# A constant's root ahead of the last boundary's first square, and a last tile stored in two halves

## The chip, the cores and the metric

The program runs on one core of a Trainium2 chip. The core has five engines that the text names: TensorE (PE in the profile, its weight loads PEld), VectorE (DVE), ScalarE (ACT), GpSimd (POOL) and SyncE (SP), which here only issues transfers. Each engine works through its own list of instructions in order; engines wait for one another by semaphores. The metric is the device time of one execution in microseconds; the time of a kernel is the median of several runs.

## The reference

Three transformer layers for one sequence of 512 tokens of width 1024 in float32: two layers with attention, a dense part and a gated embedding, then a third one whose dense part and closing normalisation are what the change lies in.

```python
def rmsnorm(x, g):
    xf = x.astype(jnp.float32)
    y = xf * lax.rsqrt(jnp.mean(xf * xf, axis=-1, keepdims=True) + NORM_EPS_2)
    return (y * g.astype(jnp.float32)).astype(x.dtype)
...
        x = x + mixed
        h2 = rmsnorm(x, norm2_g[l])
        ffn = (jax.nn.silu(h2 @ w_ffn_gate[l]) * (h2 @ w_ffn_up[l])) @ w_ffn_down[l]
        x = x + ffn
    return rmsnorm(x, norm_f_g)
```

## The kernel before

The tokens lie in four tiles of 128 (`t` = 0 to 3); `X[:, t, :]` holds the residual of tile t, one token in each partition and 1024 features in a row. All weights come in one stream of 302 chunks of 512 KB. SP loads a chunk into `RW` (L490), POOL cuts it into a high part `WH` (L529) and a low part `WL` (L532), and TensorE multiplies in three passes for each product (`mm3`, L652: high by high, high by low, low by high). Every product of the program runs through line L643.

The last stage is the downward projection of the third layer (`down`, L921): 22 chunks, one for each 128 hidden features. Its weights operand is the hidden tile (`HSH`, `HSL`, two slots each, cut by VectorE at L1688 and L1689), its moving operand the chunk. Each chunk adds to all eight banks of `PS`, two banks for each token tile. The last two chunks are treated apart (`wide_end`, L727): TensorE ends the sums of tile 0, then those of tile 1, then tile 2 with both chunks, then tile 3 with both chunks. It raises `tile_done` after each of tiles 0 to 2 and `chunk_used` after tile 3.

Then follows boundary 7, the closing normalisation, on ACT and VectorE at once. For each tile:

- VectorE adds the banks to the residual (`residual`, L1590) and raises `var_ready`;
- ACT squares the tile and sums the squares into `MV` (L2107), then takes the root of the mean square plus a small constant into `STD` (L2108), and raises `std_ready`. ACT computes functions from tables; the built program puts an instruction ACT_TABLE_LOAD where a function needs another table than the one in place. The function in use ahead of boundary 7 is Silu (L2267, in `gate`);
- VectorE takes the reciprocal of the root (`scale`, L1596), multiplies the tile by it and by the gain row `G` in place in `X` (`normed_tile`, L1610), and raises `y_ready`;
- SP waits for `y_ready` and stores the tile of 512 KB to `out` (L516); at the end it waits until all stores have landed.

VectorE's list is: residual 0, residual 1, scale 0, residual 2, scale 1, residual 3, scale 2, scale 3. ACT's is: square and root of tile 0, of tile 1, of tile 2, of tile 3.

Tiles in on-chip memory are laid out in the order in which they are declared. `X`, `XTH`, `XTL` (the operands of most other products), `RW`, `WH`, `WL` and the constants up to `IDLE` come first. `EPS`, `GAINS` and all tiles of the stages (`G`, `HT`, `HSH`, `HSL`, `OH`, `SWH`, `TWH` and others) come after `IDLE`. The built program of before puts `XTH` at byte 32,896 of each partition, `WH` at 82,048, `EPS` at 103,552, `SWH` at 108,416, `HSH` at 182,144, `HSL` at 186,240, `OH` at 209,120 and `TWH` at 217,312.

Of the kernel before, what the change touches and what calls it, by code (L numbers as in the profile page):

```python
# [26 lines left out]
P = 128  # L27
S = 512
T = S // P
D = 1024  # L30
KD = D // P
UNIT = 512
# [142 lines left out]
def program(nc, d, out):  # L175
    ctx = ExitStack()
    with ctx:
        def sb(name, shape, dt=F32, at=ctx):
            return at.enter_context(nc.sbuf_tensor(name, shape, dt))
# [5 lines left out]
        X = sb("X", [P, T, D])  # L185
# [9 lines left out]
        TRI_R = sb("TRI_R", [P, P], F32R)  # L195
        CHUNKTRI_R = sb("CHUNKTRI_R", [P, P], F32R)
        IDLE = sb("IDLE", [P, P], F32R)
        EPS = sb("EPS", [P, 2])
        GAINS = sb("GAINS", [P, 7, KD])
        BIASES = sb("BIASES", [P, 4, KD])  # L200
# [76 lines left out]
        G = sb("G", [P, 2, D], at=dense)  # L277
# [82 lines left out]
        def probs(h):  # L360
# [74 lines left out]
        y_ready = sem("y_ready")  # L435
# [36 lines left out]
        out_stored = sem("out_stored")  # L472
# [7 lines left out]

        BOUND = [(True, "layer", 0), (True, "layer", 1), (False, None, None), (True, "layer", 2),
                 (True, "layer", 3), (False, "rms", 4), (True, "rms", 5), (True, "rms", 6)]
        Y_BASE = [0, 4, 8, 12, 16, 20, 20, 20]

        @block.sync
        def _(sp):
            def load(i, j):
                if j >= RAW:
                    sp.wait_ge(lo_split, j - RAW + 1 + RAW * i)
                sp.dma_start(RW[:, j % RAW, :], d["stream"][RAW * i + j]).then_inc(landed[j % RAW], 16)  # L490


            sp.dma_start(RW[:, 0, 0:UNIT], d["stream"][0][:, 0:UNIT]).then_inc(half_landed, 16)
            sp.dma_start(RW[:, 0, UNIT:], d["stream"][0][:, UNIT:]).then_inc(landed[0], 16)
            for j in range(1, RAW):
                if j >= 2:
                    sp.wait_ge(xs_landed[j - 2], 16)
                load(0, j)
            def load_row(h):
                if h == FOX0:  # L500
                    sp.wait_ge(rows_stored, 16)
                if h >= FOX0 + 2:
                    sp.wait_ge(masked, 4 * (h - 1))
                src = d["gate_rows"][h - FOX0:h - FOX0 + 1, :].to_broadcast([P, S])
                sp.dma_start(BC[:, h % 2, :], src).then_inc(bc_landed[h % 2], 16)

            over_chunks(sp, RAW, FIRST["fox"] + 19, load)
            load_row(FOX0)
            load_row(FOX0 + 1)
            over_chunks(sp, FIRST["fox"] + 19, FIRST["out1"] + RAW, load)  # L510
            for h in range(FOX0 + 2, FOX0 + FOX_H):
                load_row(h)
            over_chunks(sp, FIRST["out1"] + RAW, CHUNKS, load)
            for t in range(T):
                sp.wait_ge(y_ready, Y_BASE[7] + t + 1)
                sp.dma_start(out[:, t, :], X[:, t, :]).then_inc(out_stored, 16)  # L516
            sp.wait_ge(out_stored, 16 * T)


        @block.gpsimd  # L520
# [832 lines left out]
        def _(ve):  # L1353
            own = Order(ve, ve_own)
            M, A, SUB, MAX, MIN = ALU.mult, ALU.add, ALU.subtract, ALU.max, ALU.min
# [13 lines left out]
            for j in range(1, 4):  # L1369
                w = slice(2 * j, 2 * j + 2)  # L1370
# [31 lines left out]
            for t in range(T):  # L1402
                x = ve.bn_stats(CBN[:, T + t, :], CQ[:, t, Q_LORA:])
            own(x)
            for j in range(8):
                x = ve.bn_aggr(CMV[:, j, :], CBN[:, j, :])
# [5 lines left out]
            for j in range(8):  # L1412
                w = slice(0, Q_LORA) if j < T else slice(Q_LORA, Q_LORA + KV_LORA)
                x = ve.tensor_scalar(CQ[:, j % T, w], CQ[:, j % T, w], CRS[:, j:j + 1], None, M)
# [157 lines left out]
            def boundary(b, end, embedding_layer=None):  # L1572
                add, kind, n = BOUND[b]
                layer = kind == "layer"

                def residual(t):
                    if add:
                        if t < T - 1:
                            ve.wait_ge(tile_done, 3 * added[0] + t + 1)
                        else:  # L1580
                            ve.wait_ge(chunk_used, end)
                        a = ALPHA if layer else 1.0
                        if layer:
                            sums = PSF[:, D * t:D * (t + 1)]
                            own(ve.scalar_tensor_tensor(sums, X[:, t, :], a, sums, M, A,  # L1585
                                                        accum_out=MV[:, t, 0:1]))
                            ve.tensor_scalar(MV[:, t, 0:1], MV[:, t, 0:1], -1.0 / D, None,
                                             M).then_inc(var_ready, 1)
                        else:
                            ve.scalar_tensor_tensor(X[:, t, :], X[:, t, :], a, PSF[:, D * t:D * (t + 1)],  # L1590
                                                    M, A).then_inc(var_ready, 1)

                def scale(t):

                    ve.wait_ge(std_ready, 4 * n + t + 1)
                    own(ve.reciprocal(RSTD[:, t:t + 1], STD[:, t:t + 1]))  # L1596
                    normed_tile(t)

                def normed_tile(t):
                    x, scale_t, done = X[:, t, :], RSTD[:, t:t + 1], last_centred if t == T - 1 else centred  # L1600
                    if layer:
                        ve.tensor_scalar(x, PSF[:, D * t:D * (t + 1)], MV[:, t, 0:1], scale_t,  # L1602
                                         A, M).then_inc(done, 1)
                    elif b < 7:
                        ve.wait_ge(var_ready, 4 * n + t + 1)
                        ve.tensor_scalar(YN[:, t, :], x, scale_t, None, M).then_inc(done, 1)
                    else:
                        ve.wait_ge(vec_landed, 144)
                        ve.wait_ge(var_ready, 4 * n + t + 1)
                        ve.scalar_tensor_tensor(x, x, scale_t, G[:, 0, :], M, M).then_inc(y_ready, 1)  # L1610

                if embedding_layer is not None:
                    ve.wait_ge(emb_hi, embedding_layer + 1)
                    ve.tensor_tensor(EL[:, :, :], ER[:, :, :], EH[:, :, :].bitcast(F32), SUB).then_inc(emb_ready, 1)
                if kind:
                    for t in range(T):
                        residual(t)
                        if t and add:
                            scale(t - 1)
                    scale(T - 1)  # L1620
                if b < 7:
                    for k in range(KD):
                        if k == 0:
                            ve.wait_ge(yt_copied, 5 * b + 4)
                            if layer:
                                own(ve.tensor_scalar(YT[:, 0, :], YT[:, 0, :], GAINS[:, n, 0:1],
                                                     BIASES[:, n, 0:1], M, A))
                            elif kind:
                                own(ve.tensor_scalar(YT[:, 0, :], YT[:, 0, :], GAINS[:, n, 0:1], None, M))
                        elif kind:  # L1630
                            ve.wait_ge(yt_ready, (KD - 1) * n + k)
                        else:
                            ve.wait_ge(yt_copied, 5 * b + 5)
                        own(ve.tensor_copy(XTH[:, k, :], YT[:, k, :]))
                        ve.tensor_tensor(XTL[:, k, :], YT[:, k, :], XTH[:, k, :].bitcast(F32),  # L1635
                                         SUB).then_inc(xt_ready, 1)
                if layer:
                    ve.wait_ge(vec_landed, 32 * (n + 1))

                    for t in range(T if embedding_layer is None else T - 2):  # L1640
                        affine(n, t)
                    if embedding_layer is None:
                        ve.wait_ge(y_ready, Y_BASE[b] + T)
                added[0] += add
# [171 lines left out]
            x = ve.scalar_tensor_tensor(ga, gl, -1.0, gl, M, MAX)  # L1816
# [12 lines left out]
            ends = by_chunk(BT[:, :, :])[:, :, :, GCH - 1:GCH]  # L1829
# [3 lines left out]
            for n, (o, src) in enumerate(((QI, QG), (KI, KG))):  # L1833
                ve.wait_ge(gla_act, n + 2)
                x = ve.tensor_tensor(o[:, :, :], o[:, :, :], src, M)
# [119 lines left out]
        def _(act):  # L1955
            own = Order(act, act_own)
            F = ACT
# [6 lines left out]
            for j in range(1, 4):  # L1964
                w = slice(2 * j, 2 * j + 2)
# [4 lines left out]
            for j in range(1, 4):  # L1970
                w = slice(2 * j, 2 * j + 2)
# [124 lines left out]
            def boundary(b):  # L2096
# [14 lines left out]
                def copy_out(t, ks=slice(0, KD)):  # L2111
# [2 lines left out]
                    src = PSF[:, o:o + D].rearrange("p (k n) -> p k n", k=KD)  # L2114
                    act.copy(YT[:, ks, t * P:(t + 1) * P], src[:, ks, :]).then_inc(yt_copied, 1)

                first_copy = T if kind and not add else 2
                for t in range(T):
                    if kind:
# [79 lines left out]
            ends = BT[:, :, :].rearrange("p f (n c) -> p f n c", c=GCH)[:, :, :, GCH - 1]  # L2199
# [197 lines left out]
```

## Time and profile before

| | |
|---|---|
| median of three runs | 1978.52 us (1976.47 to 1980.2) |
| time of the profiled execution | 1976.43 us |
| its span from first to last instruction | 1974.6 us |
| PE busy | 1945.5 us, 99% of the span |
| DVE, ACT, POOL busy | 871.2, 327.1, 1261.2 us |
| VectorE's last instruction of the boundary | starts at 1970.02, takes 1.28 us |

The times of a row are microseconds from the start of the span. The profiled execution's own time is 1.83 us above its span; what lies around the span is not in the trace. A row of the profile gives the start, the duration, the engine, the line, the operation, what it writes and reads, and in brackets how long the engine sat idle before it and what ended that.

### The profile page before, as it was taken

What the parts mean: (1) busy time and instruction counts of PE and PEld (TensorE: products, weight loads), DVE (VectorE), ACT (ScalarE), POOL (GpSimd) and SP (SyncE); (2) the same over time, 40 slices, a digit from 0 to 9 for tenths busy, and PEclk for the clock granted to TensorE, in tenths of its full rate; (3) what the DMA queues carried; (4) which work ended last, traced back from release to release, by engine and by line L of the source; (5) the groups of instructions that cost most, each with busy time, mean ns of one, the idle gap of its engine ahead of it and who ended that gap; (6) DMA issues with size and microseconds to landing.
All of it is one profiled execution on the core that took longest, in us unless ns stands there. A gap on an engine that the chain in (4) does not pass through costs nothing.

```text
span 1974.6 us, 24552 instructions
## 1 busy us (share of the span) xinstructions
PE 1945.5 (99%) x9180; PEld 1614.1 (82%) x9180; DVE 871.2 (44%) x1208; ACT 327.1 (17%) x627; POOL 1261.2 (64%) x818
## 2 busy tenths in 40 slices
PE   9999999999999999999999999999999999999998
PEld 8788788888887878888788888877888788888886
DVE  3587372253349511472832343377457840000234
ACT  1376300000003100461300000033122130000001
POOL 5586576667767547775566677756553556666674
PEclk9999999999999999999999999999999999999999
DMA  6311233333332323112233332322222233333332
GB/s 228 128 33 33 85 107 96 96 96 117 96 96 85 97 76 107 55 53 85 67 126 96 96 117 96 96 86 86 68 86 65 75 96 97 96 96 96 96 96 75
DMA packets 53698, 181.31 MB, mean 92 GB/s; under 512 B 6584, under 2 KB 9322, under 8 KB 53498
## 3 DMA queue, kind: packets, MB, share of 16 engines
q1 hardware_dynamic: 46656, 165.17, 26.6%
q10 hardware_dynamic: 6970, 15.11, 2.2%
q8 instruction: 53, 0.87, 0.2%
q14 instruction: 19, 0.16, 0.0%
HBM read 176.56 MB, written 3.70 MB: 91 GB/s over the span
## 4 chain that ended last, share of the span: by engine, by line
PE 90%; DVE 4%; POOL 3%; ACT 1%; issue 1%; POOLq 0%; DVEq 0%
PE PS L643 87%; POOL WL L532 1%; PE PS L812 1%; PE PS L891 1%; POOL WH L529 1%; POOL PB L560 1%; DVE PS L1585 0%; DVE X L1602 0%; DVE STL L1868 0%; ACT HT L2104 0%; DVE U L1930 0%; DVE STH L1867 0%; DVE ST L1877 0%; ACT PTH L2055 0%; DVE PTL L1515 0%
## 5 line engine op out<-in xcount | busy, mean ns | idle before, releaser
L532 POOL TENSOR_TENSOR WL<-RW,WH 128x1024 fp32r<-128x1024 f32 x301 | 762.5, 2533 | 25.1
L529 POOL TENSOR_SCALAR WH<-RW 128x1024 fp32r<-128x1024 f32 x301 | 352.0, 1169 | 626.3 <-PE PS L643 602.2
L643 PE MATMUL PS<-XTH,WH 128*128 128x512 f32 x1168 | 456.9, 391 | 2.1 <-DVE XTL L1635 1.6
L643 PE MATMUL PS<-XTL,WH 128*128 128x512 f32 x1168 | 454.8, 389 | 0.0
L643 PE MATMUL PS<-XTH,WL 128*128 128x512 f32 x1168 | 454.6, 389 | 0.0
L643 PE MATMUL PS<-WL,HSH 128*128 128x512 f32 x688 | 267.5, 390 | 2.1 <-POOL WL L532 2.1
L643 PE MATMUL PS<-WH,HSL 128*128 128x512 f32 x688 | 267.7, 389 | 0.0
L643 PE MATMUL PS<-WH,HSH 128*128 128x512 f32 x688 | 267.7, 389 | 0.0
L643 PEld LDWEIGHTS PS<-XTH,WH 128*128 128x128 f32 x1168 | 219.2, 188 | 50.8 <-DVE XTL L1635 3.7
L643 PEld LDWEIGHTS PS<-XTH,WL 128*128 128x128 f32 x1168 | 219.2, 188 | 46.1
L643 PEld LDWEIGHTS PS<-XTL,WH 128*128 128x128 f32 x1168 | 219.3, 188 | 43.9
L643 PE MATMUL PS<-WH,XTH 128*128 128x512 f32 (+1 forms) x480 | 182.7, 385 | 1.5 <-POOL WL L532 0.9
L643 PE MATMUL PS<-WL,XTH 128*128 128x512 f32 (+1 forms) x480 | 181.6, 383 | 0.5 <-POOL WL L532 0.5
L643 PE MATMUL PS<-WH,XTL 128*128 128x512 f32 (+1 forms) x480 | 181.5, 382 | 0.0
L1688 DVE CAST HSH<-HT 128x512 fp32r (+1 forms) x86 | 40.3, 468 | 273.9 <-PE PS L643 273.1
L643 PEld LDWEIGHTS PS<-WL,HSH 128*128 128x128 f32 x688 | 128.9, 188 | 30.1 <-POOL WL L532 3.4
L643 PEld LDWEIGHTS PS<-WH,HSH 128*128 128x128 f32 x688 | 129.1, 188 | 26.9
L643 PEld LDWEIGHTS PS<-WH,HSL 128*128 128x128 f32 x688 | 129.1, 188 | 26.8
L1650 DVE TENSOR_SCALAR HT<-PS 128x2048 f32 (+1 forms) x16 | 36.7, 2291 | 202.2 <-PE PS L643 201.5
L1689 DVE TENSOR_TENSOR HSL<-HT,HSH 128x512 fp32r<-128x512 f32 x86 | 124.0, 1441 | 3.0
L643 PEld LDWEIGHTS PS<-WH,XTH 128*128 128x128 f32 x480 | 90.0, 188 | 22.4 <-issue 4.6
L1672 DVE TENSOR_TENSOR HT<-PS,GT 128x1024 f32 (+1 forms) x11 | 13.5, 1225 | 214.7 <-ACT GT L2267 214.7
(337 smaller groups left out, 2306.0 us busy)
## 6 DMA issues: line engine op xcount, KB each, us to landing
RW<-stream SPq DMA_DIRECT2D x302, 512.0 KB, 3.6
BC<-gate_rows SPq DMA_DIRECT2D x16, 256.0 KB, 3.1
G<-gain_rows ACTq DMA_DIRECT2D x5, 512.0 KB, 3.5
X<-x ACTq DMA_DIRECT2D x1, 2048.0 KB, 12.4
G<-bias_vecs ACTq DMA_DIRECT2D x4, 512.0 KB, 5.1
out<-X SPq DMA_DIRECT2D x4, 512.0 KB, 2.7
XS<-xt ACTq DMA_DIRECT2D x3, 512.0 KB, 8.7
bias_rows<-QM ACTq DMA_DIRECT2D x1, 1536.0 KB, 6.8
```

The costliest lines, as they stand in the source:

```text
L529: pool.tensor_scalar(WH[:, j % WS, :], RW[:, j % RAW, :], 1.0, 1.0, ALU.mult, ALU.mult).then_inc(hi_split, 1)
L532: pool.tensor_tensor(WL[:, j % WS, :], RW[:, j % RAW, :], WH[:, j % WS, :].bitcast(F32), ALU.subtract).then_inc(lo_split, 1)
L560: x = pool.tensor_scalar(p, p, SM[:, s, i:i + 1], 1.0, ALU.mult, ALU.mult)
L643: return pe.matmul(o, a, b, start=start, stop=stop)
L812: x = pe.transpose(PSF[:, o:o + P], probs(h)[:, p:p + P], IDENT[:, :])
L891: x = pe.transpose(PSF[:, o:o + P], src[:, k * P:(k + 1) * P], IDENT[:, :])
L1650: ve.tensor_scalar(h, PS[:, 4 * (g % 2):4 * (g % 2) + 4, :], 0.0, None, MAX).then_inc(relued, 1)
L1672: ve.tensor_tensor(h, PS[:, bank + 2:bank + 4, :], GT[:, :, :], M).then_inc(relued, 1)
L1688: own(ve.tensor_copy(HSH[:, k % 2, :], h))
L1689: ve.tensor_tensor(HSL[:, k % 2, :], h, HSH[:, k % 2, :].bitcast(F32), SUB).then_inc(hs_ready, 1)
```

## The change

ACT computes the root of a constant in front of boundary 7's first square, into a new tile `SPARE` that nothing reads. Tile 3 is scaled in two instructions of 512 columns each, each of which raises `y_ready`, and SP stores each half by a transfer of its own. `SPARE` is declared between `IDLE` and `EPS` with 32 columns, 128 bytes in each partition, of which one column is written.

```diff
         IDLE = sb("IDLE", [P, P], F32R)
+        SPARE = sb("SPARE", [P, 32])
         EPS = sb("EPS", [P, 2])
...
+        OUT_HALVES = (slice(0, UNIT), slice(UNIT, D))
...
-            for t in range(T):
-                sp.wait_ge(y_ready, Y_BASE[7] + t + 1)
-                sp.dma_start(out[:, t, :], X[:, t, :]).then_inc(out_stored, 16)
-            sp.wait_ge(out_stored, 16 * T)
+
+            ends = [(t, slice(0, D)) for t in range(T - 1)] + [(T - 1, half) for half in OUT_HALVES]
+            for j, (t, w) in enumerate(ends):
+                sp.wait_ge(y_ready, Y_BASE[7] + j + 1)
+                sp.dma_start(out[:, t, w], X[:, t, w]).then_inc(out_stored, 16)
+            sp.wait_ge(out_stored, 16 * len(ends))
...
-                        ve.scalar_tensor_tensor(x, x, scale_t, G[:, 0, :], M, M).then_inc(y_ready, 1)
+                        for w in OUT_HALVES if t == T - 1 else (slice(0, D),):
+                            ve.scalar_tensor_tensor(X[:, t, w], X[:, t, w], scale_t, G[:, 0, w],
+                                                    M, M).then_inc(y_ready, 1)
...
+                if b == 7:
+
+                    act.activation(SPARE[:, 0:1], EPS[:, 0:1], F.Sqrt)
                 first_copy = T if kind and not add else 2
```

In the built program every tile declared behind `IDLE` lies 128 bytes further: `EPS` at 103,680, `SWH` at 108,544, `HSH` at 182,272, `HSL` at 186,368, `OH` at 209,248, `TWH` at 217,440. `X`, `XTH`, `XTL`, `RW`, `WH` and `WL` stand where they stood.

ACT's list from the end of the loop of gates (L2270) to the root of tile 1 before, in the order of the built program; GT is the gate, HT the scrap tile of the squares:

```order
L2267 ACTIVATE GT<-PS 128x1024 [waits chunk_used]
L2270 REGISTER_ALU
L2270 COMPARE_AND_BRANCH
L2107 ACTIVATE HT,MV<-X 128x1024 [waits var_ready]
L2108 ACT_TABLE_LOAD
L2108 ACTIVATE STD<-MV,EPS 128x1 [waits act_own]
L2107 ACTIVATE HT,MV<-X 128x1024 [waits var_ready]
L2108 ACTIVATE STD<-MV,EPS 128x1 [waits act_own]
```

and of the change:

```order
L2276 ACTIVATE GT<-PS 128x1024 [waits chunk_used]
L2279 REGISTER_ALU
L2279 COMPARE_AND_BRANCH
L2125 ACT_TABLE_LOAD
L2125 ACTIVATE SPARE<-EPS 128x1
L2113 ACTIVATE HT,MV<-X 128x1024 [waits var_ready]
L2114 ACTIVATE STD<-MV,EPS 128x1 [waits act_own]
L2113 ACTIVATE HT,MV<-X 128x1024 [waits var_ready]
L2114 ACTIVATE STD<-MV,EPS 128x1 [waits act_own]
```

The table load stands ahead of the wait for `var_ready` now, behind the loop, and no second one stands between the roots and the squares.

VectorE's last instructions before, from the residual of tile 3 on:

```order
L1590 SCALAR_TENSOR_TENSOR X<-X,PS 128x1024 [waits chunk_used]
L1596 RECIPROCAL RSTD<-STD 128x1 [waits std_ready]
L1610 SCALAR_TENSOR_TENSOR X<-X,RSTD,G 128x1024 [waits var_ready,vec_landed,ve_own]
L1596 RECIPROCAL RSTD<-STD 128x1 [waits std_ready]
L1610 SCALAR_TENSOR_TENSOR X<-X,RSTD,G 128x1024 [waits var_ready,vec_landed,ve_own]
```

and of the change:

```order
L1594 SCALAR_TENSOR_TENSOR X<-X,PS 128x1024 [waits chunk_used]
L1600 RECIPROCAL RSTD<-STD 128x1 [waits std_ready]
L1615 SCALAR_TENSOR_TENSOR X<-X,RSTD,G 128x1024 [waits var_ready,vec_landed,ve_own]
L1600 RECIPROCAL RSTD<-STD 128x1 [waits std_ready]
L1615 SCALAR_TENSOR_TENSOR X<-X,RSTD,G 128x512 [waits var_ready,vec_landed,ve_own]
L1615 SCALAR_TENSOR_TENSOR X<-X,RSTD,G 128x512
```

The last instruction of 1024 columns became two of 512, and the second of them waits for nothing.

## Rows read from the trace of the kernel before

**Rows 1.** The page: its first line, and shares of the chain by line.

```profile
span 1974.6 us, 24552 instructions
...
PE PS L643 87%; POOL WL L532 1%; PE PS L812 1%; PE PS L891 1%; POOL WH L529 1%; POOL PB L560 1%; DVE PS L1585 0%; DVE X L1602 0%; DVE STL L1868 0%; ACT HT L2104 0%; DVE U L1930 0%; DVE STH L1867 0%; DVE ST L1877 0%; ACT PTH L2055 0%; DVE PTL L1515 0%
```

**Rows 2.** Chain that ended last, in order of time (start, us, what).

```profile
1960.35 1.15 ACT HT L2107 x2
...
1961.52 1.28 ACT L2108
...
1962.82 0.30 ACT STD L2108
...
1963.14 0.17 DVE RSTD L1596
...
1963.34 1.24 DVE X L1610
...
1970.02 1.28 DVE X L1610
```

**Rows 3.** Timeline of ACT, 1960 us to the end.

```profile
1960.35 1.06 ACT L2107 ACTIVATE HT<-X 128x1024 f32<-128x1024 f32 x1 [114.08 <-DVE X L1590]
...
1968.31 1.06 ACT L2107 ACTIVATE HT<-X 128x1024 f32<-128x1024 f32 x1 [1.05 <-DVE X L1590]
...
1969.49 0.29 ACT L2108 ACTIVATE STD<-MV,EPS 128x1 f32<-128x1 f32 x1
```

**Rows 4.** Timeline of DVE, 1960 to 1970 us.

```profile
1960.48 1.22 DVE L1590 SCALAR_TENSOR_TENSOR X<-X,PS 128x1024 f32<-128x1024 f32 x1 [0.16 <-PE PS L643]
...
1964.54 1.21 DVE L1590 SCALAR_TENSOR_TENSOR X<-X,PS 128x1024 f32<-128x1024 f32 x1
...
1965.87 1.28 DVE L1610 SCALAR_TENSOR_TENSOR X<-X,RSTD,G 128x1024 f32<-128x1024 f32 x1
1967.07 1.21 DVE L1590 SCALAR_TENSOR_TENSOR X<-X,PS 128x1024 f32<-128x1024 f32 x1
...
1968.39 1.28 DVE L1610 SCALAR_TENSOR_TENSOR X<-X,RSTD,G 128x1024 f32<-128x1024 f32 x1
```

**Rows 5.** Timeline of PE: last product of tiles 1, 2 and 3.

```profile
1960.05 0.39 PE L643 MATMUL PS<-WH,HSL 128*128 128x512 f32 x1
...
1962.77 0.39 PE L643 MATMUL PS<-WH,HSL 128*128 128x512 f32 x1
...
1965.49 0.39 PE L643 MATMUL PS<-WH,HSL 128*128 128x512 f32 x1
```

**Rows 6.** VectorE's groups by form (busy us, mean ns): a multiplication at two widths.

```profile
L1835 DVE TENSOR_TENSOR KI<-KI,QK 128x1024 f32<-128x1024 f32 x1 | 1.2, 1217 | 0.0
...
L1902 DVE TENSOR_TENSOR OT<-OT,GG 128x512 f32<-128x512 f32 x4 | 2.8, 692 | 0.1
```

**Rows 7.** Timeline of SP: the issues of tiles 0 and 3.

```profile
1964.65 0.35 SPq L516 DMA_DIRECT2D out<-X  x1
...
1971.33 0.33 SPq L516 DMA_DIRECT2D out<-X  x1
```

**Rows 8.** Stretches of 0.5 us; last two columns: DMA engines' busy share, GB/s.

```profile
1965.50:1966.00 0.50, 0.38 (x2) 0.00 (x0) 0.47 (x3) 0.21 (x1) 0.00 (x0) 1.00 1.07 434
...
1966.50:1967.00 0.50, 0.00 (x0) 0.00 (x0) 0.50 (x1) 0.47 (x3) 0.00 (x0) 1.00 0.51 205
...
1973.50:1974.00 0.50, 0.00 (x0) 0.00 (x0) 0.00 (x0) 0.00 (x0) 0.00 (x0) 0.50 0.03 8
```

**Rows 9.** DMA issues: count, KB each, median us to landing.

```profile
BC<-gate_rows SPq DMA_DIRECT2D x16, 256.0 KB, 3.1
```

**Rows 10.** TensorE's groups by form (busy us, mean ns); PS<-moving,weights.

```profile
L643 PE MATMUL PS<-WH,HSL 128*128 128x512 f32 x688 | 267.7, 389 | 0.0
...
L643 PE MATMUL PS<-XTL,TWH 128*128 128x512 f32 x8 | 3.2, 396 | 0.0
...
L643 PE MATMUL PS<-XTL,SWH 128*128 128x512 f32 x8 | 3.1, 389 | 0.0
```

## The prediction

> **What bounds the kernel now.** I read three views, from coarse to fine. The page's shares of the chain come first: 87% of the chain that ended last is TensorE's line L643 [rows 1]. The change touches none of those products, so it can only win in what follows TensorE's last ones, or lose by moving what they read. The chain in order of time shows the end [rows 2]: ACT squares tile 0 at 1960.35, loads a table from 1961.52 to 1962.80, takes the root at 1962.82; VectorE's reciprocal follows at 1963.14, its scale at 1963.34, and the last scale runs from 1970.02 to 1971.30. The span ends at 1974.6 [rows 1]; the 3.3 us behind the last scale are the last store and the close. So the table load lies in the chain with its whole 1.28 us. The third view, the timelines of the engines, says what comes to wait when it is gone.
>
> **The root of a constant.** ACT sat idle for 114.08 us ahead of tile 0's square [rows 3]. The load and a root of about 0.3 us (as STD's in [rows 2]) fit there with 112 us to spare: price nothing. They wait for no one, and nothing on ACT stands behind them but that square. Were there no cover, they would cost 1.28 + 0.3 = 1.6 us.
>
> In the boundary I follow tile after tile, with the spacings of before. Root 0 starts at 1961.52, where the load began, and not at 1962.82: 1.30 earlier. The reciprocal moves to 1961.84 and scale 0 to 1962.04. VectorE is free, since residual 1 ends at 1960.48 + 1.22 = 1961.70 [rows 4].
>
> Residual 2 began 1.20 behind scale 0 (1963.34 to 1964.54, [rows 2, 4]), so now at 1963.24, if TensorE is done with tile 2. VectorE started tile 1 at 1960.48, 0.43 behind the start of that tile's last product at 1960.05 [rows 4, 5]. Tile 2's last product starts at 1962.77 [rows 5], so its sums are there at 1963.20: just in time, and the whole 1.30 is kept. Root 1 is no obstacle: the square of tile 1 can follow root 0, and its root starts 1.18 behind it (as 1968.31 to 1969.49, [rows 3]) and takes 0.3, so it is there by 1963.3.
>
> Scale 1 follows 1.33 behind residual 2 (1964.54 to 1965.87, [rows 4]): 1964.57. Residual 3 would follow 1.20 later, at 1965.77. Here TensorE is late: tile 3's last product starts at 1965.49 [rows 5], plus 0.43 is 1965.92. **That is the new wait:** residual 3 begins at 1965.92 and not at 1967.07 [rows 4], 1.15 earlier, and 0.15 of the 1.30 go to waiting for TensorE.
>
> From there everything follows at the old spacings: square 3 1.24 behind residual 3 (1967.07 to 1968.31, [rows 3, 4]) at 1967.16, root 3 1.18 later at 1968.34, scale 3 0.53 behind it (1969.49 to 1970.02, [rows 2, 3]) at 1968.87. Scale 2, 1.32 behind residual 3 [rows 4], runs from 1967.24 to 1968.52. By the root alone the end comes **1.15 us** sooner. It is worth nothing at the least, were ACT not what ends last, and 1.30 at the most.
>
> **The last tile in halves.** No scale of 512 columns stands in the trace. A multiplication of 1024 columns took 1217 ns and one of 512 columns 692 [rows 6], 525 ns less, so a half takes 1.28 - 0.53 = 0.76 us. Two instructions in a row overlap by 0.08 (scale of 1.28 us, next one after 1.20). The first half runs from 1968.87 to 1969.63, the second from 1969.55 to 1970.31. A whole scale would end at 1970.15: VectorE **pays 0.16**.
>
> For the stores I take three rows. SP issues 0.03 behind VectorE's end (1971.30 to 1971.33, [rows 2, 7]). The first bytes move 0.85 behind the issue (1964.65 to 1965.50, from where on the stretches are full, [rows 7, 8]). The 512 KB of tile 0 fill one and a half stretches of 0.5 us and a little at 410 to 434 GB/s [rows 8]; 524,288 bytes at some 415 GB/s are 1.26 us. Before, tile 3's bytes run from 1972.18 to 1973.44, which fits the share of 0.03 in the stretch from 1973.50 [rows 8].
>
> After the change, tile 2 is issued at 1968.55 and its bytes move from 1969.40 to 1970.66. The first half is issued at 1969.66, could start at 1970.51 and stands behind tile 2 till 1970.66; its bytes end at 1971.29. The second half is issued at 1970.34, could start at 1971.19 and stands behind the first till 1971.29: it ends at 1971.92. That is 1.52 before 1973.44. By the root alone tile 3 would end at 1972.29. So the halves **bring 0.37**, with VectorE's 0.16 already paid, and the transfer engines are busy without a gap from 1969.40 to the end. SP's second issue costs nothing: it takes 0.35 [rows 7], and SP is free at 1970.01.
>
> The unknown is how fast pieces of 2 KB move (a half row of each partition, where a whole row is 4 KB). If they cost by bytes, the sum stands; without any queue behind tile 2 the second half ends at 1971.82, 1.6 in all. The nearest row against it: `BC`, 256 KB in rows of 2 KB, needed 3.1 us to land [rows 9]. Less 0.85, 2.25 for each half, one behind the other from 1970.66, would end at 1975.16, 1.7 later than before. I take the cost by bytes, since `BC` reads one row of memory 128 times and the stores write 128 different ones.
>
> The Trainium skill ("DMA: Bandwidth & Descriptors", section "Anatomy of one DMA — SWDGE (gpsimd) path") gives a transfer a fixed part of about 2.0 us and a part by size at 436 GB/s, which speaks for halving only the last one's 0.6 us. By that rule, an estimate, the halves bring 0.60 - 0.16 = 0.44 and the sum is 1.59. It counts no transfer ahead in line, which these rows show.
>
> **Tiles that move by 128 bytes.** I cost this at nothing, on a row: `TWH`, which starts 32 bytes behind a multiple of 64, makes a product of 396 ns; `SWH`, which starts at a multiple of 64, one of 389 [rows 10]. What costs there is the place within 64 bytes, and a step of 128 keeps it. But `HSH` goes from 128 behind a multiple of 256 to a multiple of 256, and no weights of before start at such a place. As bounds I take the 7 ns of [rows 10] with either sign on all 3 x 688 = 2064 products with `HSH` or `HSL`: 14.4 us more or less.
>
> **Sum.** 1.15 + 0.37 = 1.5 us off the profiled execution: span 1974.6 to 1973.1, own time 1976.43 to 1974.9. The median of the runs shown, 1978.52, stands 2.1 above that execution; the same 1.5 off it gives **1977.0 us**, 0.08% faster. A difference under 0.2%, 4.0 us, is about what a measurement of this kernel can't tell from no change, and the tail has no 4 us to give.
>
> **Rivals.**
> - *The halves lose, the root wins.* Pieces of 2 KB move slower than by bytes. For it speaks `BC`, against it that it reads and doesn't write. From 1977.5 (root alone less 0.16) to 1980.2 (the bound above); I put it at 1977.9.
> - *The load doesn't leave the chain*, because a second one is needed in the boundary. Against it: the squares stood between roots without another load (at tile 3 the root starts 1.18 behind its square, the time of the square alone, [rows 3]), and the order of the changed program shows one load. Then the halves alone remain, 0.4: 1978.1.
> - *Slower: the moved weights.* If a start at a multiple of 256 costs `HSH` and `HSL` what the start of `TWH` costs, the three down projections pay 7 ns on 2064 products: 1977.0 + 14.4 = 1991.4. It decides against the change from 4.0 us + 1.5 us = 5.5 over 2064, 2.7 ns a product.
> - *Faster by the same door.* If such a start is better than the present one by as much: 1962.6. From 1.2 ns a product on it would be seen.
>
> **How the numbers follow.** Forecast as summed, 0.71; the halves lose, 0.15; the load stays, 0.05; moved weights slower, 0.05; moved weights faster, 0.04. The first three are all within 0.2%; from each side I give 0.01 to 0.02 for the scatter of a median (the three runs shown span 3.7 us). So faster 0.06, same 0.88, slower 0.06. The forecast's bounds alone are 1976.9 to 1977.4. The range takes in the scatter, 1.9 to either side, and the losing halves: **1974.9 to 1979.8**; it leaves out the two cases of the moved weights and the worst of `BC`.
>
> **What would show it.** On ACT a table load and a root by 1848, and none behind 1960; square to root 0 within 1.2 us. Residual 3 idle for about 0.15 on TensorE, at 0.43 behind its last product. Scale 3 as two instructions of 0.76, the second 0.68 behind the first. Five stores, the last three with no gap between their bytes. Some 2.8 us from VectorE's end to the span's, where it was 3.3, since less is left to move when VectorE ends. A product with `HSH` of other than 389 ns, or halves that land later than tile 3 did, would make the prediction wrong.

## The result and the profile after

The changed kernel takes **1990.19 us** (median of four runs, 1989.34 to 1991.42); the kernel before takes 1978.66 beside it (four runs, 1976.47 to 1980.2). The ratio is 1.0057, interval 1.0044 to 1.0069: it is **slower by 11.5 us**, 0.57%. The prediction, 1977.0 in a range of 1974.9 to 1979.8, was wrong; the time lies 1.2 us from its rival with the moved weights, 1991.4, which had a chance of 0.05.

The page of the changed kernel first: its first line, the engines' busy time and the shares of the chain by line. The profiled execution took 1989.34 us in all.

```profile
span 1987.5 us, 24555 instructions
...
PE 1960.2 (99%) x9180; PEld 1617.9 (81%) x9180; DVE 870.3 (44%) x1209; ACT 327.5 (16%) x628; POOL 1262.0 (63%) x818
...
PE PS L647 88%; PE PS L816 1%; POOL WL L536 1%; PE PS L895 1%; POOL WH L533 1%; POOL PB L564 1%; DVE STL L1874 0%; DVE X L1606 0%; DVE PS L1589 0%; DVE STH L1873 0%; DVE ST L1883 0%; DVE U L1936 0%; ACT HT L2110 0%; ACT HT L2121 0%; ACT PTH L2061 0%
```

The chain has the shape of [rows 1]: TensorE's products (L643 there, L647 here) hold it. The number of products is the same, 9180, but TensorE is busy for 1960.2 us where it was 1945.5. The engines beside it kept their times within 1 us. So the products themselves became slower, and the next view, TensorE's groups by form (busy us, mean ns; moving operand, then weights), says which; it answers to [rows 10].

```profile
L647 PE MATMUL PS<-XTH,WL 128*128 128x512 f32 x1168 | 454.8, 389 | 0.0
...
L647 PE MATMUL PS<-WH,HSL 128*128 128x512 f32 x688 | 271.5, 395 | 0.0
L647 PE MATMUL PS<-WH,HSH 128*128 128x512 f32 x688 | 271.5, 395 | 0.0
L647 PE MATMUL PS<-WL,HSH 128*128 128x512 f32 x688 | 271.3, 395 | 1.8 <-POOL WL L536 1.8
...
L647 PE MATMUL PS<-XTH,SWH 128*128 128x512 f32 x8 | 3.2, 396 | 0.0
...
L647 PE MATMUL PS<-XTL,SWH 128*128 128x512 f32 x8 | 3.2, 395 | 0.0
```

Each of the three groups with `HSH` or `HSL` went from 389 or 390 ns to 395, and `SWH`, the row on which the prediction rested, from 389 to 395. Products of tiles that stand ahead of `SPARE` (`XTH`, `WL`) stayed at 389. The three groups' busy times grew by 3.8 us each, 11.4 together. Most of the rest of the 14.7 is no part of the loss: the products of `IDLE` with itself took 41.7 us before and 43.7 in the change, but also 43.7 in the first experiment's kernel, which lost nothing.

The tail did what was forecast. ACT's timeline, which answers to [rows 2, 3]:

```profile
1857.94 1.28 ACT L2125 ACT_TABLE_LOAD   x1
1859.24 0.20 ACT L2125 ACTIVATE SPARE<-EPS 128x1 f32<-128x1 f32 x1
...
1974.75 1.06 ACT L2113 ACTIVATE HT<-X 128x1024 f32<-128x1024 f32 x1 [115.31 <-DVE X L1594]
...
1975.93 0.30 ACT L2114 ACTIVATE STD<-MV,EPS 128x1 f32<-128x1 f32 x1
```

VectorE's timeline, which answers to [rows 2, 4], from the first residual on:

```profile
1973.49 1.22 DVE L1594 SCALAR_TENSOR_TENSOR X<-X,PS 128x1024 f32<-128x1024 f32 x1 [3.07 <-PE PS L647]
...
1976.46 1.29 DVE L1615 SCALAR_TENSOR_TENSOR X<-X,RSTD,G 128x1024 f32<-128x1024 f32 x1
...
1980.47 1.22 DVE L1594 SCALAR_TENSOR_TENSOR X<-X,PS 128x1024 f32<-128x1024 f32 x1 [0.17 <-PE PS L647]
...
1983.43 1.41 DVE L1615 SCALAR_TENSOR_TENSOR X<-X,RSTD,G 128x512 f32<-128x512 f32 x2
```

TensorE's timeline, the last product of tile 3 (see [rows 5]):

```profile
1980.03 0.40 PE L647 MATMUL PS<-WH,HSL 128*128 128x512 f32 x1
```

And the stretches of 0.5 us in which the last stores move (last two columns: the share of the DMA engines, GB/s), which answer to [rows 8]:

```profile
1984.00:1984.50 0.50, 0.00 (x0) 0.00 (x0) 0.50 (x2) 0.00 (x0) 0.00 (x0) 0.50 1.01 410
1984.50:1985.00 0.50, 0.00 (x0) 0.00 (x0) 0.34 (x1) 0.00 (x0) 0.00 (x0) 0.50 1.00 393
...
1985.50:1986.00 0.50, 0.00 (x0) 0.00 (x0) 0.00 (x0) 0.00 (x0) 0.00 (x0) 0.50 0.98 377
1986.00:1986.50 0.50, 0.00 (x0) 0.00 (x0) 0.00 (x0) 0.00 (x0) 0.00 (x0) 0.50 0.98 381
1986.50:1987.00 0.50, 0.00 (x0) 0.00 (x0) 0.00 (x0) 0.00 (x0) 0.00 (x0) 0.50 0.27 98
```

The load and its root stand a hundred microseconds ahead of the boundary; tile 0's root follows its square at once. The tail before began with this row of VectorE's timeline:

```profile
1959.10 1.22 DVE L1590 SCALAR_TENSOR_TENSOR X<-X,PS 128x1024 f32<-128x1024 f32 x1 [3.06 <-PE PS L643]
```

From the first residual to the end of the span it is 1987.5 - 1973.49 = 14.01 us. Before, it was 1974.6 - 1959.10 = 15.50. The tail became 1.49 us shorter, and it began 14.39 later. From the first residual to the end is the measure of the tail in what follows: it leaves out all that comes ahead, whose scatter is larger than the tail's whole gain (the runs of the kernel before lie 3.7 us apart).

### The profile page after: what moved, and what is told of

The parts are those of the page before. It is cut to its first block, busy times and chain, and to the rows that moved or that the text cites. A ratio compares the mean times of both kernels' runs of the same rounds, so it can differ in the third digit from the quotient of the medians.

```text
span 1987.5 us, 24555 instructions
## 1 busy us (share of the span) xinstructions
PE 1960.2 (99%) x9180; PEld 1617.9 (81%) x9180; DVE 870.3 (44%) x1209; ACT 327.5 (16%) x628; POOL 1262.0 (63%) x818
## 4 chain that ended last, share of the span: by engine, by line
PE 91%; DVE 4%; POOL 3%; ACT 1%; issue 1%; POOLq 0%; DVEq 0%
PE PS L647 88%; PE PS L816 1%; POOL WL L536 1%; PE PS L895 1%; POOL WH L533 1%; POOL PB L564 1%; DVE STL L1874 0%; DVE X L1606 0%; DVE PS L1589 0%; DVE STH L1873 0%; DVE ST L1883 0%; DVE U L1936 0%; ACT HT L2110 0%; ACT HT L2121 0%; ACT PTH L2061 0%
## 5 line engine op out<-in xcount | busy, mean ns | idle before, releaser
L647 PE MATMUL PS<-XTH,WH 128*128 128x512 f32 x1168 | 456.8, 391 | 2.1 <-DVE XTL L1641 1.6
L647 PE MATMUL PS<-XTH,WL 128*128 128x512 f32 x1168 | 454.8, 389 | 0.0
L647 PE MATMUL PS<-XTL,WH 128*128 128x512 f32 x1168 | 454.6, 389 | 0.0
L647 PE MATMUL PS<-WL,HSH 128*128 128x512 f32 x688 | 271.3, 395 | 1.8 <-POOL WL L536 1.8
L647 PE MATMUL PS<-WH,HSL 128*128 128x512 f32 x688 | 271.5, 395 | 0.0
L647 PE MATMUL PS<-WH,HSH 128*128 128x512 f32 x688 | 271.5, 395 | 0.0
L647 PEld LDWEIGHTS PS<-XTH,WH 128*128 128x128 f32 x1168 | 219.2, 188 | 50.9 <-DVE XTL L1641 3.7
L647 PEld LDWEIGHTS PS<-XTH,WL 128*128 128x128 f32 x1168 | 219.2, 188 | 45.8
L647 PEld LDWEIGHTS PS<-XTL,WH 128*128 128x128 f32 x1168 | 219.3, 188 | 44.0
L647 PE MATMUL PS<-WH,XTH 128*128 128x512 f32 (+1 forms) x480 | 182.7, 385 | 1.3 <-PE PS L647 0.6
L647 PE MATMUL PS<-WL,XTH 128*128 128x512 f32 (+1 forms) x480 | 181.4, 383 | 0.5 <-POOL WL L536 0.5
L647 PE MATMUL PS<-WH,XTL 128*128 128x512 f32 (+1 forms) x480 | 181.6, 382 | 0.0
L647 PEld LDWEIGHTS PS<-WL,HSH 128*128 128x128 f32 x688 | 129.4, 188 | 33.1 <-POOL WL L536 3.1
L647 PEld LDWEIGHTS PS<-WH,HSL 128*128 128x128 f32 x688 | 129.6, 188 | 30.5
L647 PEld LDWEIGHTS PS<-WH,HSH 128*128 128x128 f32 x688 | 129.6, 188 | 30.2
L647 PEld LDWEIGHTS PS<-WH,XTH 128*128 128x128 f32 x480 | 90.0, 188 | 22.2 <-issue 4.4
```

The costliest lines, as they stand in the source:

```text
L647: return pe.matmul(o, a, b, start=start, stop=stop)
```

## The experiments

Three theories stood at the start. **Place of the weights to the moving operand**: `HSH` and `HSL` moved by 128 bytes and the chunk did not, and a product whose two operands start at different places within a stretch of 256 bytes is slower. **Place of the weights alone**: a start at a multiple of 256 is slow, whatever the other operand does. **Another cause**: the root, the halves or their waits cost the time, and the slower products are a by-product of it. `XTH`, `XTL`, `WH` and `WL` start 128 bytes behind a multiple of 256 in the kernel before, and so do `HSH`, `HSL` and `SWH`; `OH` and `TWH` start 224 behind one.

**A step of 256 bytes.** The change, with a larger `SPARE`:

```diff
-        SPARE = sb("SPARE", [P, 32])
+        SPARE = sb("SPARE", [P, 64])
```

> The change with the spare tile 64 columns wide, so that all tiles behind it move by 256 bytes and not by 128. If the place of the weights within 256 bytes made the loss, HSH and HSL start 128 behind a multiple of 256 again, their products are back at 389 to 390 ns, and the time is 1977 us, 1.5 below the kernel before. If any move costs, or the place within 512 bytes counts, they stay at 395 and the time at 1990. If the new instructions themselves made the loss (the root, the second scale, the fifth store), it is 1990 with products at 395 too.

Measured: 1977.69 us (ten runs, 1977.19 to 1978.85) against 1979.22 of before, ratio 0.9994, interval 0.9984 to 1.0003. Nothing but the size of a tile that nobody reads turned 11.5 us slower into no change. TensorE's groups:

```profile
L647 PE MATMUL PS<-WH,HSH 128*128 128x512 f32 x688 | 267.7, 389 | 0.0
L647 PE MATMUL PS<-WH,HSL 128*128 128x512 f32 x688 | 267.6, 389 | 0.0
```

The root and the halves are both in this kernel, so the theory of another cause falls. The tail took 1975.5 - 1961.61 = 13.89 us. VectorE's timeline, its first residual and its last scale:

```profile
1961.61 1.22 DVE L1594 SCALAR_TENSOR_TENSOR X<-X,PS 128x1024 f32<-128x1024 f32 x1 [3.06 <-PE PS L647]
...
1971.38 1.41 DVE L1615 SCALAR_TENSOR_TENSOR X<-X,RSTD,G 128x512 f32<-128x512 f32 x2
```

`HSH` now starts at byte 182,400; what this place has in common with that of before, 182,144, is the remainder by 256.

**The place alone.** The kernel before with one tile that nothing reads or writes:

```diff
         IDLE = sb("IDLE", [P, P], F32R)
+        SPARE = sb("SPARE", [P, 32])
         EPS = sb("EPS", [P, 2])
```

> The kernel before with nothing but an unused tile of 128 bytes declared ahead of EPS: no root, no halves. If the place makes the loss, products with HSH and HSL take 395 ns and the time is 1978.6 + 14.4 = 1993 us, and the tail from VectorE's first residual to the end of the span is 15.5 us as before. If the new instructions make the loss, the time is that of the kernel before, 1978.6.

Measured: 1992.0 us (four runs, 1990.84 to 1993.6), ratio 1.0067, interval 1.005 to 1.0084. No instruction is added, removed or moved, and it costs 1992.0 - 1979.22 = 12.8 us:

```profile
L644 PE MATMUL PS<-WH,HSL 128*128 128x512 f32 x688 | 271.5, 395 | 0.0
```

The three groups with `HSH` and `HSL` grew by 11.3 us in all, 5.5 ns for each of their 2064 products. The smaller tiles behind `IDLE` moved as well, and their products of 512 columns with the chunks or with `XTH` and `XTL` (those of `CTH`, `EH`, `SWH` and their low parts, less a little for `OH`) add some 1.0 us. The tail took 15.5 us, as before. So 12.8 from the place and 1.5 back from the tail make 11.3; measured were 11.5.

**Everything moved together.** The change, with `SPARE` ahead of `X` and not behind `IDLE`. Every tile then starts 128 bytes further, and both operands of the products with `HSH` stand at multiples of 256 (`WH` at 82,176, `HSH` at 182,272).

```diff
+        SPARE = sb("SPARE", [P, 32])
         X = sb("X", [P, T, D])
...
-        SPARE = sb("SPARE", [P, 32])
```

> The change with the spare tile of 128 bytes declared ahead of X: X, XTH, XTL, RW, WH, WL and all others move by 128 bytes together, HSH is again at a multiple of 256, and so are XTH and WH. If a product is slow by the place of its weights alone, all large products are slow (2064 with HSH, 3504 with WH or WL, 1248 with XTH or XTL as weights, 6.3 to 7 ns each): about 2021 us. If it is slow where weights and moving operand start at different places within 256 bytes, none is slow: 389 to 390 ns, 1977 us.

Measured: 1977.22 us (ten runs, 1974.69 to 1978.18), ratio 0.9989, interval 0.9979 to 0.9999.

```profile
L647 PE MATMUL PS<-XTL,WH 128*128 128x512 f32 x1168 | 455.5, 390 | 0.0
...
L647 PE MATMUL PS<-WH,HSL 128*128 128x512 f32 x688 | 267.7, 389 | 0.0
```

`HSH` and `HSL` start exactly where they start in the slow kernel, and are fast. The theory of the weights' own place falls; the place to the moving operand stands.

**The chunks moved.** If that theory holds, moving `RW`, `WH`, `WL` and all behind them must slow the other products, those of chunks with `XTH` and `XTL`, and leave `HSH` and `HSL` fast:

```diff
         XTL = sb("XTL", [P, KD, S], F32R)
+        SPARE = sb("SPARE", [P, 32])
         RW = sb("RW", [P, RAW, CHUNK])
...
-        SPARE = sb("SPARE", [P, 32])
```

> The change with the spare tile declared between XTL and RW: RW, WH, WL, HSH and HSL move by 128 bytes, XTH and XTL don't. By the place of the weights alone: products with HSH (395 ns) and with WH or WL as weights (395) are slow, those with XTH or XTL as weights fast (389 to 391), 5568 x 6.5 ns, about 2013 us. By the place of the weights relative to the moving operand: products with HSH are fast (389; HSH and WH moved together), and all products of XTH with WH, either way round, are slow (395), 4752 x 6.5 ns, about 2008 us.

Measured: 2002.52 us (four runs, 2000.27 to 2002.71), ratio 1.0117, interval 1.01 to 1.0134.

```profile
L647 PE MATMUL PS<-XTL,WH 128*128 128x512 f32 x1168 | 461.3, 395 | 0.0
...
L647 PE MATMUL PS<-WH,HSL 128*128 128x512 f32 x688 | 267.7, 389 | 0.0
...
L647 PE MATMUL PS<-WH,XTL 128*128 128x512 f32 x416 | 164.2, 395 | 0.0
```

The groups changed sides, whichever of the two operands is the weights and whichever moves. Against 1977.22 of everything moved, which ran beside it, it is 25.3 us on 3 x 1168 + 3 x 416 = 4752 products, 5.3 ns each. The size was expected too large, at 6.5 ns; the sign and the groups were right.

**Smaller steps.** The change with `SPARE` of 16 columns (64 bytes) and of 8 columns (32 bytes):

```diff
-        SPARE = sb("SPARE", [P, 32])
+        SPARE = sb("SPARE", [P, 16])
```

> The change with a spare tile of 64 bytes: HSH starts 64 bytes further than WH within 256, OH 160 further. If equal places within 256 bytes are needed, both stay at 395 and the time is 1990. If only a distance of 128 (and of 32 and 96) costs, HSH is at 389 and the time near 1977.5. Equal places within 64 bytes alone can't be the rule, since 128 costs.

Measured: 1991.4 us (one run; before on the same chip 1978.74).

> The change with a spare tile of 32 bytes: HSH starts 32 bytes further than WH within 256, OH at a distance of 128. If equal places within 256 bytes are needed, both are slow (395 to 397 ns) and the time is 1990 or a little more; a shift that is no multiple of 64 may cost more than one of 64 or 128, since OH at a distance of 96 took 396 to 397 and HSH at 128 took 395.

Measured: 1992.07 us (one run). TensorE's groups of the two, the step of 64 first:

```profile
L647 PE MATMUL PS<-WH,HSL 128*128 128x512 f32 x688 | 272.1, 395 | 0.0
```

```profile
L647 PE MATMUL PS<-WH,HSL 128*128 128x512 f32 x688 | 272.1, 396 | 0.0
```

So 32, 64 and 128 bytes of difference cost the same, 6 to 7 ns, and `TWH` with 96 in [rows 10] costs 7. There is no slope; the two places are equal or they are not. Nor do 512 bytes count: against `WH` at 128 behind a multiple of 512, `HSH` at 384 behind one (before) and at 128 (the step of 256) both took 389.

**No tile.** The root of the constant goes into a column of `STD` that boundary 7 overwrites later, so nothing moves:

```diff
-        SPARE = sb("SPARE", [P, 32])
...
-                    act.activation(SPARE[:, 0:1], EPS[:, 0:1], F.Sqrt)
+                    act.activation(STD[:, 0:1], EPS[:, 0:1], F.Sqrt)
```

> The root of the constant is written to STD's first column, which root 0 overwrites, and there is no spare tile; halves as in the change. Nothing moves. If place alone made the loss, products with HSH are at 389 to 390 ns, and the tail from VectorE's first residual to the end of the span takes 14.0 us against 15.5 before: 1.5 us below the kernel before, ratio 0.9992. If the new instructions cost elsewhere, the ratio is above 1.

Measured: 1977.34 us (11 runs, 1974.81 to 1978.31) against 1978.74 of before, ratio 0.9992, interval 0.9983 to 1.0001. The tail took 1976.1 - 1962.20 = 13.9 us. This is what the change was forecast to be, and the forecast was 1977.0. The gain in the whole time, 1.4 us, is no larger than the scatter (the interval reaches 1.0001); that it is there rests on the tail.

**The third layer's tiles in place too.** As the kernel without the tile, and three gaps that put `OH`, `OL`, `TWH` and the other weights of that stage 128 behind a multiple of 256:

```diff
         U = sb("U", [P, T, S + 2], at=third)
+        sb("GAP_A", [P, 40], at=third)
         CV = sb("CV", [P, T, S], at=third)
...
+        sb("GAP_B", [P, 48], at=third)
         ST = sb("ST", [P, 2, 2 * DV], at=third)
...
+        sb("GAP_C", [P, 16], at=third)
         decays = ExitStack()
```

> As the run without a spare tile, and three unused gaps of 160, 192 and 64 bytes in the third layer's tiles, which put OH, OL, TWH, TWL, QIH, KIH, QEH, STH, KTH and others at 128 behind a multiple of 256, where WH and XTH stand. By relative place: 96 products with OH or OL go from 396 to 390 ns, 24 with TWH or TWL too, 120 x 6.3 ns = 0.8 us, some more from the small products of the third layer, which wait anyway: 0.8 to 1 us below the run without the gaps. If only the place within 64 bytes counted for these, the same; if place doesn't count for them, 396 stays.

Measured: 1976.72 us (11 runs, 1975.89 to 1977.89), ratio 0.999, interval 0.9981 to 0.9999: the fastest of all, though its lead of 0.6 over the kernel without the gaps lies inside the scatter. What shows the effect are the groups, those without the gaps first:

```profile
L646 PE MATMUL PS<-WH,OL 128*128 128x512 f32 x32 | 12.7, 397 | 0.0
L646 PE MATMUL PS<-XTL,TWH 128*128 128x512 f32 x8 | 3.2, 396 | 0.0
```

and with them:

```profile
L649 PE MATMUL PS<-WH,OL 128*128 128x512 f32 x32 | 12.5, 390 | 0.0
...
L649 PE MATMUL PS<-XTL,TWH 128*128 128x512 f32 x8 | 3.1, 389 | 0.0
```

A placement that was slow in the kernel before was made fast, by the same rule.

**The root alone**, in `STD`, with tile 3 scaled and stored whole:

```diff
-        OUT_HALVES = (slice(0, UNIT), slice(UNIT, D))
+        OUT_HALVES = (slice(0, D),)
```

> Nothing moves; the root of the constant is written to STD's first column, the last tile is scaled and stored whole. By the prediction's working the last scale starts 9.77 us behind the first residual (10.92 before), residual 3 idles 0.15 on TensorE, and from the first residual to the end of the span it is 15.5 - 1.15 = 14.35 us.

Measured: 1977.21 us (one run; before on the same chip 1979.9, one run too). VectorE's timeline, residual 0, residual 3 and the last scale:

```profile
1961.29 1.22 DVE L1593 SCALAR_TENSOR_TENSOR X<-X,PS 128x1024 f32<-128x1024 f32 x1 [3.06 <-PE PS L646]
...
1968.10 1.22 DVE L1593 SCALAR_TENSOR_TENSOR X<-X,PS 128x1024 f32<-128x1024 f32 x1
...
1971.06 1.28 DVE L1614 SCALAR_TENSOR_TENSOR X<-X,RSTD,G 128x1024 f32<-128x1024 f32 x1
```

The last scale starts 9.77 us behind the first residual; before it was 1970.02 - 1959.10 = 10.92. That is the 1.15 of the prediction. The tail took 1975.4 - 1961.29 = 14.11, 1.39 shorter than before: 0.24 of it lies behind the last scale.

**The halves alone**, with nothing in front of the first square and no `SPARE`, so nothing moved:

```diff
-                if b == 7:
-
-                    act.activation(SPARE[:, 0:1], EPS[:, 0:1], F.Sqrt)
```

> Nothing moves; no root of a constant, so the table load stays behind tile 0's square; the last tile in two halves. The last scale starts 10.92 us behind the first residual as before, VectorE ends 0.13 to 0.16 later, and from the first residual to the end of the span it is 15.5 - 0.4 = 15.1 us. If halves cost the transfers more than by bytes, it is 15.5 or more.

Measured: 1979.03 us (one run), tail 1977.2 - 1961.61 = 15.59: not 15.1, but 0.1 longer than before. The halves alone bring nothing. The stretches at its end:

```profile
1975.50:1976.00 0.50, 0.00 (x0) 0.00 (x0) 0.00 (x0) 0.00 (x0) 0.00 (x0) 0.50 0.51 189
1976.00:1976.50 0.50, 0.00 (x0) 0.00 (x0) 0.00 (x0) 0.00 (x0) 0.00 (x0) 0.50 0.05 20
```

Most of the store is through in the first of the two stretches, and a small rest comes behind at 20 GB/s. The transfers from 1974.00 to its end by queue and kind (packets, MB, share of 16 engines):

```profile
q1 hardware_dynamic: 338, 0.66, 54.0%
q14 instruction: 1, 0.01, 0.6%
```

One packet of the queue for instructions lies among those of the stores. The kernel before has one such packet in its tail as well; the tails of the root alone, of the kernel without the tile and of the change have none. There it comes within a microsecond behind the start of the table load, about 1858.5 in the change, while before and in the halves alone it comes some 10 us behind it, near 1971.9 and 1974.4. So with the root ahead the packet leaves the tail together with the load. That the packet is what holds the store's rest back is argued from that, and so is its part in the 0.24 above; no run moved the packet alone.

## Why the prediction was wrong

**The step that failed** is "Tiles that move by 128 bytes. I cost this at nothing, on a row". The row was right: `TWH` costs 396 and `SWH` 389. The reading was not: "What costs there is the place within 64 bytes, and a step of 128 keeps it". `SWH` and `TWH` differ in their remainder by 64 and also in their remainder by 256, and the row could not tell these apart. `SWH` was fast because it starts 128 behind a multiple of 256, as `XTH` and `XTL` do, and the step of 128 took that away from it and from `HSH` and `HSL`. [Rows 10] and the addresses beside them had the rule in them: `SWH` and `HSL`, at 389, stand at the place of their moving operand within 256 bytes, `TWH`, at 396, stands 96 bytes off. I looked at the weights' addresses alone and not at both operands of a product.

**The bound held, and the rival's time nearly came.** 7 ns on 2064 products was priced at 14.4 us; the place alone cost 12.8, of which these products have 11.3, 5.5 ns each. The rival was given 0.05, since its mechanism was put as a place at which no weights of before start. That mechanism was wrong too: at just that place, with the chunks moved along, `HSL` took 389.

**The root.** The term was 1.15, and the root alone gave 1.15 to the last scale. In the change itself it gave less: the last scale starts 1983.43 - 1973.49 = 9.94 behind the first residual, 0.98 sooner than before. The reason is the slower products again: the last product of tile 3 starts 6.54 behind the first residual where it was 1965.49 - 1959.10 = 6.39 [rows 5], and residual 3 waits for it, 0.44 behind its start, as forecast (0.43); its idle time of 0.17 was forecast as 0.15. With the step of 256 bytes, where the products are fast, the last scale starts 1971.38 - 1961.61 = 9.77 behind the first residual, 1.15 sooner, with both edits in place. The Trainium skill ("ScalarE: Activation LUTs", section "What ACT_TABLE_LOAD costs") gives a load about 1.28 us and a drain of about 1.38 more. The trace agrees with the first, 1.28 in [rows 2] and after; of a drain no row shows anything: where the load stands in the chain, the root starts 0.02 behind its end in [rows 2] and 0.01 in the halves alone (1964.04 + 1.28 to 1965.33).

**The halves.** The widths came out as forecast: two scales in 1.41 us, where 0.68 + 0.76 = 1.44 was put. The cost by bytes held nearly: in the change the two full stretches of half rows alone have 377 and 381 GB/s, those of tile 2's whole rows 410 and 393, and `BC`'s slow landing did not return. VectorE's end to the span's end is 2.66, forecast 2.8. But the term of 0.37 is not one number. Alone the halves bring nothing (15.59 against 15.50); with the root, they take the tail from 14.11 to between 13.68 and 13.90 in the five kernels that have both edits and fast products of `HSH`, 0.21 to 0.43. Behind the last scale's start the change gained 0.51 (1974.6 - 1970.02 = 4.58 before, 1987.5 - 1983.43 = 4.07 now), but 0.24 came there with the root alone, so some 0.27 is left for the halves. That the sum of the tail, 1.5, was hit in the change (1.49) is luck in part: 0.98 stood for 1.15 and 0.51 for 0.37, off by some 0.15 each in opposite directions, and the 0.24 was in no term.

**What stays open** is why a product is slower when its two operands start at different places within 256 bytes. The runs show that it is so, for the products of 512 columns with a chunk or with `XTH` and `XTL`, for either operand as the weights and for every difference tried. The mean duration of a product is all that the trace has of it. The groups that moved account for some 12.3 of the 12.8 us; the rest lies inside the scatter.

## What to carry to other kernels

A tile that nothing reads can be the costliest line of a change: before adding one, list the start addresses of the built program, before and after, for both operands of each product, and keep them at equal remainders by 256, with padding to 256 bytes or by reusing a column that is there. A difference between two rows can come from anything in which the rows differ; where a term of 14 us hangs on it, the kernel with the place alone, one declared tile, costs one run. A short tail is measured from an event inside it, not from the start of the span, where the scatter is larger than what it can give.

## What the runs showed of the hardware

- In the large groups with a chunk, a product of 128x512 takes 389 to 390 ns (391 to 392 for `XTH` with `WH`) when weights and moving operand start at the same place within 256 bytes of a partition, and 395 to 397 when they don't, with differences of 32, 64, 96 and 128 bytes alike. The weight loads took 188 to 189 ns in the slow kernels and in the fast ones. The Trainium skill ("SBUF — State Buffer", section "Operand start alignment") says of the start addresses what is legal and that nothing was timed there; all of these places are legal, and they differ by 12.8 us here.
- TensorE's granted clock is no part of that: over the whole span it was 0.999 of full speed (the level of 2.4 GHz) in the kernel before, 0.998 in the change and in the fast kernel with the step of 256. In a stretch of downward projections it is 1.00 before and in the change, with 231 products in 52 us before and 226 after (columns from the left: us; busy time and count of PE, PEld, DVE, ACT and POOL; clock; share of the DMA engines; GB/s):

```profile
418.00:470.00 52.00, 52.00 (x231) 43.06 (x230) 24.14 (x20) 0.98 (x1) 37.20 (x20) 1.00 0.37 122
```

```profile
419.00:471.00 52.00, 52.00 (x226) 42.16 (x225) 23.04 (x20) 0.00 (x0) 35.70 (x19) 1.00 0.36 113
```

- Products of 256 columns did not show it: the gaps took `STH` and `QEL` from different places to equal ones, and their group went from 279 to 281 ns. Nor did two other kinds: with the chunks moved, the products of 384 columns with `WH` and `XTL` took 337 ns for 336, and the few of 512 columns and 96 rows with `XTH` and `AQH` took 395 ns before and 394 in the change, which moved `AQH` by 128 bytes. So the rule is one for products of 512 columns and 128 rows, as far as these runs go, and no group of a few products is good to the nanosecond: `PTL` with `AVH`, 24 products whose operands moved together, took 393 before and 395 in the change.
- In the change's tail, pieces of 2 KB leave at 377 to 381 GB/s, rows of 4 KB at 393 to 410.
- Transfers of instructions show beside the stores: a single packet of 0.01 MB lies in the last 3 us of the kernel before and of the halves alone, and none in the tails of the kernels whose table load stands ahead of the boundary.
